# Mixture of experts at the end of a two-block model: expert outputs through DRAM instead of scatter matmuls

## What is computed

```python
# D_MODEL 1024, SEQ 256, 16 experts of width 512, two per token, both of one group
p_top, g_idx = lax.top_k(softmax(t @ rg_w + rg_b), 1)
e_top, e_idx = lax.top_k(softmax(e_logits), 2)
gate = ...                                   # (tokens, 16), two entries of a row are not zero
for e in range(N_EXPERTS):
    hid = jax.nn.silu(t @ w1[e]) * (t @ w3[e])
    out = out + gate[:, e:e + 1] * (hid @ w2[e])
x = x + g_f[:, None] * out
```

## Time and profile before

| | us |
|---|---|
| median of 3 runs | 1749.94 |
| the three runs | 1749.81, 1749.94, 1755.15 |
| profiled execution, its time | 1754.62 |
| profiled execution, its span | 1752.5 |
| PE busy in it | 1636.6 (93%) |
| DVE busy in it | 1168.7 (67%) |
| ACT busy in it | 909.3 (52%) |

### The profile page before, as it was taken

How to read it: one execution, slowest core, us unless ns; L and a number is a source line. 1 busy time by engine, 2 the same in 40 slices (tenths; PEclk the granted TensorE clock), 3 DMA queues, 4 the chain that set the end, 5 groups by cost and what they waited for, 6 DMA issues and landing times.

```text
span 1752.5 us, 20738 instructions
## 1 busy us (share of the span) xinstructions
PE 1636.6 (93%) x8208; PEld 1335.3 (76%) x8208; DVE 1168.7 (67%) x1655; ACT 909.3 (52%) x1401; POOL 40.7 (2%) x46
## 2 busy tenths in 40 slices
PE   7999999999999999999998999997997679999998
PEld 7987788776888798778877678886665567787786
DVE  7457656646545774766674788665655569999997
ACT  5475543434444455744443553433534447777784
POOL 0010000000000001000000000001100000000000
PEclk9999999999999999999999999998988889999999
DMA  7444235516555453523453578743420238888884
GB/s 275 169 168 178 87 120 192 196 69 242 191 192 186 173 195 145 213 97 120 166 205 134 218 265 311 276 154 144 162 73 29 72 118 301 320 324 324 309 309 182
DMA packets 48747, 333.18 MB, mean 190 GB/s; under 512 B 6146, under 2 KB 6788, under 8 KB 9860
## 3 DMA queue, kind: packets, MB, share of 16 engines
q1 hardware_dynamic: 48644, 331.79, 51.4%
HBM read 330.72 MB, written 1.05 MB: 189 GB/s over the span
## 4 chain that ended last, share of the span: by engine, by line
PE 72%; DVE 16%; ACT 6%; DMA 3%; issue 1%; POOL 1%; DVEq 0%; SPq 0%; ACTq 0%
PE bank L197 69%; DVE wls L209 6%; PE bank L201 4%; DMA raw<-in_ws_dram 3%; ACT whs L205 2%; ACT arena L206 1%; DVE arena L209 1%; DVE sm L220 1%; DVE h L209 1%; POOL sm L229 1%; DVE P1l L209 1%; DVE arena L217 1%; DVE arena L824 1%; DVE P0l L209 1%; ACT arena L205 1%
## 5 line engine op out<-in xcount | busy, mean ns | idle before, releaser
L209 DVE TENSOR_TENSOR wls<-raw,whs 128x1024 fp32r<-128x1024 f32 x490 | 582.2, 1226 | 259.7 <-ACT whs L205 257.8
L205 ACT ACTIVATE whs<-raw 128x1024 fp32r<-128x1024 f32 x490 | 493.9, 1053 | 289.8 <-PE bank L197 193.8
L197 PE MATMUL bank<-whs,P0h 128*128 128x512 f32 (+1 forms) x896 | 359.8, 402 | 9.4 <-DVE arena L217 3.4
L197 PE MATMUL bank<-whs,P0l 128*128 128x512 f32 (+1 forms) x896 | 350.6, 391 | 0.0
L197 PE MATMUL bank<-wls,P0h 128*128 128x512 f32 (+1 forms) x896 | 350.0, 391 | 0.0
L197 PE MATMUL bank<-whs,P1h 128*128 128x512 f32 (+1 forms) x536 | 212.9, 397 | 5.4 <-DVE arena L209 3.0
L197 PEld LDWEIGHTS bank<-whs,P0h 128*128 128x128 f32 x896 | 169.8, 189 | 57.7 <-DVE arena L217 7.8
L197 PE MATMUL bank<-whs,P1l 128*128 128x512 f32 (+1 forms) x536 | 208.6, 389 | 0.0
L197 PE MATMUL bank<-wls,P1h 128*128 128x512 f32 (+1 forms) x536 | 208.5, 389 | 0.0
L197 PEld LDWEIGHTS bank<-whs,P0l 128*128 128x128 f32 x896 | 169.6, 189 | 36.6
L197 PEld LDWEIGHTS bank<-wls,P0h 128*128 128x128 f32 x896 | 170.0, 190 | 32.3
(11 more groups left out here) (242 smaller groups left out, 2313.7 us busy)
## 6 DMA issues: line engine op xcount, KB each, us to landing
raw<-in_ws_dram SPq DMA_DIRECT2D x302, 1024.0 KB, 4.8
lnb<-in_ln_g_dram SPq DMA_DIRECT2D x6, 512.0 KB, 5.8
lnb<-in_ln_b_dram SPq DMA_DIRECT2D x6, 512.0 KB, 6.5
mid<-in_bias_dram SPq DMA_DIRECT2D x1, 2048.0 KB, 7.7
h<-in_x_dram SPq DMA_DIRECT2D x2, 512.0 KB, 3.9
lnb<-in_mem_dram SPq DMA_DIRECT2D x1, 1024.0 KB, 13.2
memT<-in_ctx_dram SPq DMA_DIRECT2D x1, 1024.0 KB, 7.8
lnb<-in_b_ada_dram SPq DMA_DIRECT2D x2, 512.0 KB, 6.8
```

What stands on the lines that cost most here:

```text
L197: return PE.put(lambda e: e.matmul(out, lhsT, rhs, start=start, stop=stop, skip_group_check=skip), w, inc)
L205: return AC.put(lambda e: e.activation(out, in_, func, bias=bias, scale=scale), w)
L209: return VE.put(lambda e: e.tensor_tensor(out, a, b, op), w)
```

## The change

Experts 0 to 13 (`NFAR` = 14) are no longer scattered by matmuls. Their output leaves PSUM by one ScalarE copy per 128x512 half in plain float32 (no low part, no gate weight in it), and GpSimd issues a DMA of 512 KB that writes it to a DRAM tensor `ydram`. `places` computes on VectorE, once, for each token the two rows of `ydram` and the two gate weights. After the pick of the last expert and the last write GpSimd issues four indirect DMAs (`fetch`, 128 rows of 4 KB each), and `combine` forms the weighted sum on VectorE and adds it to `h`. Experts 14 and 15 still go through one-hot and scatter.

The loop runs over 32 chunks: up(c), down(c - 1), with the weight stream in that order. Odd experts' tokens go to `P1` and even ones to `P0`, so `pick(e)` waits for `up(e - 2)`. The key of the split slots' choice is changed, so that a slot never used before is taken last. GpSimd now has its own branch, and its two memsets stand behind it.

```diff
@@ split_half
-                j = min(ready_, key=lambda j: -1 if used[j] is None else used[j])
+                j = min(ready_, key=lambda j: NU if used[j] is None else used[j])
@@ sparse: new functions
+            def places():
+                at, hit = smv(144, 32), smv(456, 32)
...
+                v = ts(base, iota[:, 0:16], 128.0, None, ALU.mult, None, v_slot, c_cst)
+                v = tt(at3, mask.rearrange("p (t e) -> p t e", t=2), bcast_mid(base, 2), ALU.mult, v)
...
+                for i in range(4):
+                    T["idx", i] = vcopy(idx[i][:, :], both[:, i:i + 1], v)
+            def write(e):
+                GP.wait([T["y", e, 0], T["y", e, 1]])
+                GP.items.append(lambda g: g.dma_start(yd[e * 128:(e + 1) * 128, :], Y[e % 2][:, :]).then_inc(s_y[e % 2], 16))
+                T["wr", e] = (s_y[e % 2], 16 * (e // 2 + 1))
+            def fetch():
+                for i in range(4):
+                    GP.wait([T["wr", NFAR - 1], T["wr", NFAR - 2], T["idx", i], T["x", NEXP - 1, 0], T["x", NEXP - 1, 1]])
+                    GP.items.append(lambda g, i=i: g.indirect_dma_start(
+                        far[i], None, yd[:, :], bass.IndirectOffsetOnAxis(ap=idx[i][:, :], axis=0)).then_inc(s_g[i], 16))
+            def combine():
+                for t in range(2):
+                    a, b = far[t], far[2 + t]
+                    v = ts(a, a, share[:, t:t + 1], None, ALU.mult, None, (s_g[t], 16), T["share"])
+                    v = stt(b, b, share[:, 2 + t:3 + t], a, ALU.mult, ALU.add, (s_g[2 + t], 16), v)
+                    v = tt(b, b, gab[:, 1, :], ALU.mult, v, A["rows", 1])
+                    T["h", t] = tt(h[:, t, :], h[:, t, :], b, ALU.add, v)
@@ down
-                    if c:
-                        v = split(part(Y[e % 2], slice(None), cols_), banks[b][:, :], m, free=[start, g_("sc", e - 2)])
+                    if i and e < NFAR:
+                        v = act(Y[e % 2][:, cols_], banks[b][:, :], ACT.Copy, m, start, g_("wr", e - 2))
+                    elif i:
+                        v = split(part(Yp, slice(None), cols_), banks[b][:, :], m, free=[start, g_("sc", e - 1)])
...
+                if i and e < NFAR:
+                    write(e)
@@ the loop
-            for e in range(NEXP):
-                up(e, 0)
-                up(e, 1)
+            for c in range(2 * NEXP):
+                e = c // 2
+                up(c)
+                if c == 2:
+                    places()
...
                 feed(1)
-                down(e, 0)
-                turn_hidden(e, 1)
-                if e:
-                    scatter(e - 1)
+                if c:
+                    down(c - 1)
                 feed(1)
-                if e + 1 < NEXP:
+                if c % 2 and 2 <= e + 1 < NEXP:
                     pick(e + 1)
...
+                if c == 2 * NFAR + 1:
+                    fetch()
+            combine()
+            turn_hidden(2 * NEXP - 1)
+            scatter(NFAR)
+            down(2 * NEXP - 1)
             scatter(NEXP - 1)
```

More of the change, by code:

```diff
@@ L22 @@
 NEXP = 16
+NFAR = NEXP - 2
 NEG = -1e30
@@ L61, in mlp @@
                     plan.append(("w_ada_2", 0, 512 * (i % 2), 512, ((512 * beside[i // 2], 512),)))
-            if split and c % 2:
-                down(c - 1)
-                down(c)
-        if split is None:
-            down(n - 1)
+        down(n - 1)
     for l in range(DEPTH):
@@ L1179, in up_chunk @@
                     if t == 1:
-                        if c == nch - 1 and not paired:
+                        if c == nch - 1 and held:
                             state["hold"] = True
@@ L1198, in down_chunk @@
                         done[("acc", t, hf)] = m
-                    if t == 0 and c == nch - 1 and not paired:
+                    if t == 0 and c == nch - 1 and held:
                         turn_hidden(c)
-                        feed(2)
+                        feed(4)
                 done[("B", c - 1)] = m
@@ L1207, in mlp @@
                 up_chunk(c)
-                if not paired and c:
+                if c:
                     down_chunk(c)
-                if paired and c % 2:
-                    down_chunk(c)
-                    down_chunk(c + 1)
-            if not paired:
-                down_chunk(nch)
+            down_chunk(nch)
             L["P1"] = PE.last()
@@ L1734, in gather, with x_of @@
                     T["all", k] = v
-                T["zero"] = z
+                T["zero"], T["rows"] = z, m
+            def x_of(e):
+                return P1 if e % 2 else P0
             begin_at = {}
@@ new lines, in sparse @@
+            share = smv(664, 4)
+            far = [arr(2432 + 1024 * i, 1024) for i in range(3)] + [memT[:, 0:4, :].rearrange("p a b -> p (a b)")]
+            def write(e):
[7 more added lines that the diff above has]
+                        far[i], None, yd[:, :], bass.IndirectOffsetOnAxis(ap=idx[i][:, :], axis=0)).then_inc(s_g[i], 16))
@@ L1769, in turn_onehot @@
                 T["PT", e] = m
-                a = act(back(e % 2), banks[7][:, 256:512].rearrange("p (a b) -> p a b", a=2), ACT.Copy, m, start,
-                        g_("sc", e - 2))
+                a = act(back(e % 2), banks[7][:, 256:512].rearrange("p (a b) -> p a b", a=2), ACT.Copy, m, start)
                 T["B", e] = a
@@ L1920, in _ @@
         def _(e):
-            for f in GP.items:
-                f(e)
+            run(e, 4)
         @block.tensor
```

113 lines of the change are left out of this document (69 added, 44 removed).

## The result

The changed kernel takes 1828.83 us (median of 4 runs, 1823.21 to 1829.6). The kernel before took 1752.55 us on the same chip. The ratio is 1.0436 with a 95% interval of 1.0417 to 1.0456: the change is 76 us slower, where 10.5 us faster was forecast and the range ended at 1758. The profiled execution, 1823.21 us, is the fastest of the four; its span is 1821.4 us, 69 more than that of the profiled execution before.

A forecast was written before the change was run, and what follows sets the result against it. TensorE was taken to set the period of 19.85 us an expert, with VectorE and DMAs close behind. Terms -23.1 + 4.5 + 2 + 6.4 - 0.3 = -10.5 took the median 1749.94 to 1739.4 us, range 1721 to 1758.

The forecast's parts named there:

- The loop, -23.1: Experts' loop: period falls from 19.85 to 18.2 us, over 14 experts a gain of 23.1 us.
- VectorE's part: Experts' loop: VectorE's work falls from 18.3 to 16.6 us an expert, its 1.4 us of waits stay.
- The ring: Three raw slots for weight loads: a round of 8.3 us at best fits 9.1 us at a period of 18.2.
- VectorE's count says 18.0: Experts' loop: 16.6 us of VectorE work plus 1.4 us of waits give a period of 18.0 us.
- I add 0.2 for the writes: Experts' loop: the writes of expert outputs to DRAM add 0.2 us to the period, taken as 18.2.
- the write that holds up a weight unit by d: Rival, chance 0.14: each write delays a weight unit by d; from 1.0 us the gain is gone, time up to 1762.5.
- TensorE's floor, 17.0 us: Experts' loop: without scatter and one-hot group TensorE alone would need 17.0 us an expert, down from 19.4.
- the transfers' 17.6 us at 387 GB/s: Experts' loop: an expert's loads and write, 6.82 MB, take 17.6 us at the full-queue rate.
- The floor case: Rival, chance 0.20: VectorE's waits overlap its work and the loop reaches TensorE's floor, time 1722.6.
- The router, +4.5: Router's two softmaxes: a weight half between exponential and sum delays each by 2.25 us, costing 4.5 us.
- places +2: Second expert: eighteen tiny VectorE operations, 3.6 us of work, cost 2 us.
- the end +6.4: After the last multiply: combine takes 8.2 us, TensorE waits 4.9 us and restarts at a slower clock, costing 6.4 us.

The follow-up runs named there:

- e1: Changed kernel with one condition altered, so that the next expert's pick stands one chunk earlier: 1775.64 us, ratio 1.0143.
- a4: Changed kernel as it is, late pick included, with a fourth raw slot alone: 1801.95 us, ratio 1.0273.
- e16: Changed kernel with the pick one chunk earlier and a fourth raw slot, turn and combine where the change put them: 1748.99 us, ratio 0.9978.
- b4: Kernel before with a fourth raw slot in the experts' part and nothing else: 1745.15 us, ratio 0.9955.
- e14: Changed kernel with pick one chunk earlier, turn ahead of up, combine split in two places and a fourth raw slot, all writes kept: 1727.65 us, ratio 0.9851.
- e4: Changed kernel with the old key for the choice of a split slot, an unused slot taken first again: 1826.47 us, ratio 1.0427.
- bw: Kernel before with only 14 writes of 512 KB from GpSimd to DRAM added, which nobody reads: 1762.56 us, ratio 1.0067.
- e8: Changed kernel with the pick one chunk earlier and without places, fetch and combine, writes kept: 1763.71 us, ratio 1.0067.
- e6: Changed kernel with DRAM outputs kept but weight stream and loop in the earlier order (up, up, down, down): 1783.28 us, ratio 1.0206.

## Why the prediction was wrong, point by point

- **The loop, -23.1: it was some +61,** from its start to the last multiply (1796.69 - 1424.69 = 372.0 us for 1735.43 - 1424.87 = 310.6). Two steps failed. The first is under "VectorE's part": "the new order gives transposed values more slack". It looked at the way from the multiply to the turn and not at another value that TensorE takes from VectorE, the pick. Before, the pick stood ahead of the second down, with its 12 matmuls and the one-hot group behind; the change puts it directly ahead of the up that needs it and behind weight halves. Worth 53 us, shown by one condition (e1), and by a4 against e16 that it is the order and not the loads. By the prediction's own way of counting, with the row of each operation at hand, a deadline for the pick would have given this as an estimate: half, pick high part, pick low part in a row behind a full TensorE, 1.06 + 1.14 + 0.83 = 3.0 us and the slow start, every expert. The waits in a4 (3.20 us in the rows above) are this row of three; in the changed kernel the late loads come on top.
- **The ring: "It fits, barely".** The second step that failed. 8.3 us for a slot's round were set against 9.1 us at a period of 18.2. The round at best is not what a slot gets: with three slots a period of 18.63 (no writes) is a round of 18.63 / 2 = 9.3 us, and with writes 20.36 / 2 = 10.2 us, since halves queue on ScalarE behind output copies and picks, and loads land later beside writes. With four slots the ring allows 1.33 times that, and the loop ran at 17.49. The earlier trace rows had shown ScalarE waiting for loads 17.3 us of 258 at a period of 19.85: the ring was already touched, and in b4 the fourth slot gave back 7 us (period 19.47). The removal of work from TensorE was priced by work counts, "VectorE's count says 18.0"; a count has no round in it.
- **The turn.** "The new order gives transposed values more slack" counts the matmuls between a multiply and its turn. What ran short is the stretch behind the turn: the low part stands behind a weight half on VectorE, and 12 matmuls later the down needs it. The first of an expert's two turns had that place before; the second, which had the scatter's 8 matmuls and the pick behind it, was moved there. The place costs 11 us with three slots and 17 with four.
- **Writes: "I add 0.2 for the writes",** to the period of an expert. With three slots 12 to 19 us in all, 0.8 to 1.6 us each. The rival that named this mechanism, the write that holds up a weight unit by d and decides from d = 1.0 us, had the right place and about the right size, and a chance of 0.14. It still gave only 1762.5.
- **TensorE's floor, 17.0 us,** was nearly right: with the ring open 17.45 to 17.49 us, with writes and without. That the transfers' 17.6 us at 387 GB/s came out too is a coincidence: without writes they had room and the period stayed. The floor case's 1722.6 is 5 us from e14's 1727.65. But it is reached by another kernel than the one forecast.
- **The router, +4.5: right.** Each sum came 2.1 us behind its exponential, 4.2 us in all (e4). The 4.0 us by which the exponential stood earlier in the profiled execution are there with the old key too, and in `bw`, which has nothing of the change: executions of the same code differ by this much. In the profiled execution this spread happens to hide the cost.
- **places +2 and the end +6.4: right in kind, 3.6 us too small.** Leaving out places, fetch and combine gave 12 us (e8) against 8.4. Combine took 9.15 us for 8.2: the operations hardly overlap, and the scalar_tensor_tensor takes 1.28 for 1.14. TensorE waited 5.68 us, and the 12 matmuls behind took 4.6 us (1806.23 to 1810.83) instead of 2.75. The fetch was on time.
- **Left open:** the order of before with DRAM outputs (e6) is 32 us slower than the kernel before. Writes, places and combine account for some 24 to 27 of it. The rest would be TensorE's missing cover for the turn, which was not tried alone there.

## What to carry to other kernels

When work is taken from the engine that is full, list every value that it takes from the others, those that do not move included, and for each what stands ahead of it in its engine's in-order stream: a step on which the full engine depends must not stand behind one that waits for the full engine. Count a ring of buffers by its real round (period x slots / units, read from the trace), and ask what period it allows before you price a saving by work counts. And try the buffer first: one more slot moved the same kernel from 13.5 us slower than the kernel before to 25 us faster, while it gave that kernel only 7.

## What the runs showed of the hardware

- A DMA's landing time is not its price. In e14 loads landed after 7.1 us, the latest of all runs, and writes after 8.5 us, and it is the fastest. In bw the writes landed after 3.2 us and cost 12 us. The issues of e14 from 1465 to 1700:

```profile
raw<-in_ws_dram SPq DMA_DIRECT2D x78, 1024.0 KB, 7.1
ydram<-Y POOLq DMA_DIRECT2D x13, 512.0 KB, 8.5
```

- The transfers kept over 50 us what the earlier trace rows showed for 5, and more. A window of e14:

```profile
1564.00:1614.00 50.00, 49.62 (x221) 39.86 (x220) 47.05 (x52) 43.46 (x59) 1.60 (x3) 1.00 1.00 402
```

  The Trainium skill, HBM Reference, Specifications, gives an effective 358 GB/s per core. Estimated by it, this loop takes 19.0 us an expert; 17.49 was measured, and that decides. The same page has about 425 for a core that streams alone, as this one does. That stands above the 402, and the fullest slices of 5.9 us of e14 reach it (up to 430).
- By the fit of the Trainium skill, DMA: Bandwidth & Descriptors, section on the GpSimd path, a DMA of 512 KB from GpSimd is estimated at 3.2 us. The trace agrees in bw (3.2) and not beside a fuller queue (6.8 in the changed kernel, 8.5 in e14). Issued by ScalarE's hardware queue the writes cost the same.
- A TensorE that waits once an expert, 4.5 to 6.0 us in the changed kernel, has its granted clock at 0.90 in the mean there, and the matmuls behind a wait start 0.43 us apart at first: about 1.5 us more for each wait, which neither the waits nor the busy time name as lost. Behind the 3.20 us of a4 it is as much.
